# Where the attention's band mask is added to the scores: VectorE, in place in PSUM, in the stead of TensorE products

## The reference, cut to what matters

```python
valid = (jnp.abs(q_pos[:, None] - k_pos[None, :]) <= WINDOW) & (k_pos >= 0) & (k_pos < S)
s_win = jnp.einsum('bqkgd,bnkd->bkgqn', qb, kb).astype(jnp.float32) * scale
s_win = jnp.where(valid, s_win, MASK_VALUE)
s_ctx = jnp.einsum('bqkgd,bckd->bkgqc', qb, k_ctx).astype(jnp.float32) * scale
probs = sink_softmax(jnp.concatenate([s_ctx, s_win], axis=-1), sink)
o = (jnp.einsum('bkgqc,bckd->bqkgd', probs[..., :n_ctx], v_ctx.astype(jnp.float32))
     + jnp.einsum('bkgqn,bnkd->bqkgd', probs[..., n_ctx:], vb.astype(jnp.float32)))
```

## Time and profile before

| | |
|---|---|
| median of 3 runs | 2247.52 us (2244.53 to 2247.78) |
| the profiled execution's own time | 2246.7 us |
| its span, first to last instruction | 2245.1 us |
| PE busy | 2146.2 us (96%) |
| DVE busy | 1493.3 us (67%) |
| ACT busy | 1131.6 us (50%) |
| POOL busy | 368.8 us (16%) |
| attention, from its first scores to its last values | about 130.7 to 284.3 us |

### The profile page before, as it was taken

The page is one execution under the profiler, slowest core; times in us unless marked ns, Lnnn a source line. Parts: engine busy times, 40 slices in busy tenths (PEclk is TensorE's granted clock), DMA queues, the critical chain, the costliest instruction groups (busy, mean ns, idle before and its releaser), DMA issues.

```text
span 2245.1 us, 33136 instructions
## 1 busy us (share of the span) xinstructions
PE 2146.2 (96%) x12156; PEld 1715.7 (76%) x12157; DVE 1493.3 (67%) x1391; ACT 1131.6 (50%) x1278; POOL 368.8 (16%) x247
## 2 busy tenths in 40 slices
PE   6999999999999999799799999999999999999994
PEld 4876688887888888678677788888888887666882
DVE  3456656667457544789566645459999997555984
ACT  4135536222224522377555534347888885445872
POOL 0030004999991000100000000000000000000001
PEclk8999999999999999799899999999999999999997
DMA  8472022555443222399577755559999996557974
GB/s 328 195 293 83 1 97 100 188 189 200 168 179 120 76 93 102 142 375 371 197 275 271 306 197 184 193 183 410 367 395 378 384 370 251 211 218 269 380 292 158
DMA packets 78098, 515.87 MB, mean 230 GB/s; under 512 B 9008, under 2 KB 9264, under 8 KB 20944
## 3 DMA queue, kind: packets, MB, share of 16 engines
q1 hardware_dynamic: 61696, 442.85, 51.3%
q0 software_dynamic: 16336, 72.11, 8.5%
HBM read 482.41 MB, written 32.51 MB: 229 GB/s over the span
## 4 chain that ended last, share of the span: by engine, by line
PE 88%; DVE 6%; issue 2%; ACT 1%; DMA 1%; SPq 0%; POOL 0%; DVEq 0%; ACTq 0%; POOLq 0%
PE ps L1851 25%; PE ps L1853 24%; PE ps L1852 24%; PE ps L2232 3%; PE ps L2296 2%; PE ps L603 2%; PE ps L558 2%; PE ps L614 2%; PE ps L2278 1%; DVE lo L1191 1%; PE ps L1910 1%; PE ps L562 1%; DVE fl L1495 1%; DMA raw_pair<-w_mod 1%; PE ps L2029 0%
## 5 line engine op out<-in xcount | busy, mean ns | idle before, releaser
L1851 PE MATMUL ps<-ah,hi 128*128 128x512 f32 (+1 forms) x768 | 286.8, 373 | 5.7 <-DVE al L1356 2.4
L1853 PE MATMUL ps<-ah,lo 128*128 128x512 f32 (+1 forms) x768 | 284.9, 371 | 0.0
L1852 PE MATMUL ps<-al,hi 128*128 128x512 f32 (+1 forms) x768 | 284.9, 371 | 0.0
L1439 DVE TENSOR_TENSOR lo<-raw,hi 128x2048 fp32r<-128x2048 f32 x112 | 255.8, 2284 | 0.0
L1439 DVE TENSOR_TENSOR loa<-raw_pair,hia 128x2048 fp32r<-128x2048 f32 x112 | 251.1, 2283 | 1.1 <-ACT hia L960 1.1
L1439 DVE TENSOR_TENSOR lob<-raw_pair,hib 128x2048 fp32r<-128x2048 f32 x112 | 251.7, 2283 | 0.0
L960 ACT ACTIVATE hia<-raw_pair 128x2048 fp32r<-128x2048 f32 x112 | 214.4, 1915 | 49.9 <-DMA raw_pair<-w_moe 49.8
L1191 DVE TENSOR_TENSOR lo<-raw_pair,hi 128x2048 fp32r<-128x2048 f32 x59 | 183.8, 3118 | 80.0 <-ACT hi L848 78.5
L960 ACT ACTIVATE hi<-raw 128x2048 fp32r<-128x2048 f32 x112 | 214.8, 1918 | 11.1 <-DMA raw<-w_moe 11.1
L1851 PE MATMUL ps<-hia,xth 128*128 128x512 f32 x504 | 204.2, 405 | 16.2 <-issue 14.6
L960 ACT ACTIVATE hib<-raw_pair 128x2048 fp32r<-128x2048 f32 x112 | 215.0, 1921 | 1.0 <-DMA raw_pair<-w_moe 0.9
(11 more groups left out here) (309 smaller groups left out, 4050.0 us busy)
## 6 DMA issues: line engine op xcount, KB each, us to landing
raw_pair<-w_moe SPq DMA_DIRECT2D x224, 1024.0 KB, 6.7
raw<-w_moe SPq DMA_DIRECT2D x112, 1024.0 KB, 6.8
raw_pair<-w_pre SPq DMA_DIRECT2D x59, 1024.0 KB, 4.8
raw_pair<-w_mod SPq DMA_DIRECT2D x20, 1024.0 KB, 7.2
raw_pair<-w_mod POOLq DMA_DIRECT2D x14, 1024.0 KB, 5.2
rawm<-w_mod POOLq DMA_DIRECT2D x14, 1024.0 KB, 5.5
dispatched_x<-zt POOLq DMA_DIRECT2D x22, 512.0 KB, 10.8
xg<-dispatched_x POOLq DMA_DIRECT2D x8, 1024.0 KB, 11.3
```

What stands on the lines that cost most here:

```text
L1439: dve.tensor_tensor(LO_OF[j], raw8(r), HI_OF[j].bitcast(F32), ALU.subtract).then_inc(raw_used[r], 1)
L1851: pe.matmul(outp, wh, ah, start=first, stop=False, skip_group_check=True)
L1852: pe.matmul(outp, wh, al, start=False, stop=False, skip_group_check=True)
L1853: return pe.matmul(outp, wl, ah, start=False, stop=last, skip_group_check=True)
```

## The change

The identity `IDR`, its ACT copy and the mask products are gone from PE. The mask tile becomes plain fp32. DVE adds it in place in PSUM to the left and right chunks of both heads, with one TENSOR_TENSOR per pair before the maximum: 128x512 elements in a middle block, 128x256 in an edge block, the mask broadcast over the two heads. In middle blocks head 0 now has its window keys in the order left, mid, right (before: left, right, mid), so that the four masked chunks have a regular stride; the scores that PE starts with there are the right chunk's. The copy of the last two transposes (middle blocks) moves from DVE to ACT, behind the two exponentials of its step and ahead of `es`, `rrow` and `ah`. The semaphore counts follow.

```diff
         def attention_act(act, first_done):
...
                         act.activation(PR[2 * (q % 2) + f][:, 0:BLK * n_keys(q)], score_head(q, f), ACT.Exp,
                                        bias=NM[:, h:h + 1], scale=SCALE, accum_out=LSUM[:, h:h + 1]).then_inc(pr_ready, 1)
+                if 0 <= p < NPAIR and len(turns(p)) == 3:
+                    act.wait_ge(pt_full, turns_before(p) + 3)
+                    act.activation(PTS[p % 2][:, 8:10, :], turned(8, 10), ACT.Copy).then_inc(pta_ready, 1)
...
         def attention_dve(dve, tn, late):
...
-                    for g, (a, b) in enumerate(turns(p)[1:]):
-                        dve.wait_ge(pt_full, turns_before(p) + 2 + g)
-                        dve.tensor_copy(PTS[p % 2][:, a:b, :], turned(a, b)).then_inc(ptd_ready, 1)
+                    dve.wait_ge(pt_full, turns_before(p) + 2)
+                    dve.tensor_copy(PTS[p % 2][:, 4:8, :], turned(4, 8)).then_inc(ptd_ready, 1)
...
+                    if not edge(s // 8):
+                        dve.wait_ge(window_full, s - 7)
                     dve.wait_ge(s_full, s + 1)
+                    link(dve.tensor_tensor(masked_at(s), masked_at(s), masks_for(s), ALU.add))
                     link(dve.tensor_reduce(NRM[:, cols_], score_pair(s), AX.X, ALU.max, negate=True))
...
         def attention_pe(pe, second_done):
...
-                def masked(outs, sides):
-                    return pe.matmul(outs, IDR[:], MASK[:, sides], start=False, stop=True, skip_group_check=True)
...
                     for f in range(2):
-                        part(f, 2, 2, win_keys)
-                    side = slice(BLK, 2 * BLK) if b == 0 else slice(0, BLK)
-                    for f in range(2):
-                        at = score_at(s, f, 3 if b == 0 else 2)
-                        ins = masked(PSF[:, at:at + BLK], side)
+                        ins = part(f, 2, 2, win_keys)
                 else:
-                    part(0, 4, 1, K[:, kp, b * BLK:(b + 1) * BLK]).then_inc(mid_done, 1)
+                    part(0, 4, 1, win_keys[:, 2 * BLK:3 * BLK]).then_inc(right_done, 1)
                     part(1, 3, 2, ctx_keys)
                     part(0, 0, 2, ctx_keys)
-                    pe.wait_ge(mid_done, s - 7)
-                    part(1, 0, 3, win_keys)
-                    part(0, 2, 2, win_keys.rearrange("p (c n) -> p c n", c=3)[:, 0:3:2, :])
-                    at = score_at(s, 0, 2)
-                    masked(PSF[:, at:at + 2 * BLK], slice(0, 2 * BLK))
-                    at = score_at(s, 1, 0)
-                    ins = masked(PSF[:, at:at + 3 * BLK].rearrange("p (c n) -> p c n", c=3)[:, 0:3:2, :],
-                                 slice(0, 2 * BLK))
+                    pe.wait_ge(right_done, s - 7)
+                    part(1, 0, 3, win_keys).then_inc(window_full, 1)
+                    ins = part(0, 2, 2, win_keys[:, 0:2 * BLK])
```

More of the change, by code:

```diff
@@ L168, in program @@
         SILC = put("silc", [P, KD, 2], F32)
-        IDR = put("idr", [P, P], F32R)
         NRM = put("nrm", [P, NH], F32)
@@ L185, in program @@
         VC = put("vc", [P, 2, 256], F32, r2 + 26624)
-        MASK = put("mask", [P, 2 * BLK], F32R, r2 + 28672)
+        MASK = put("mask", [P, 2 * BLK], F32, r2 + 28672)
         PR = [put(f"pr{i}", [P, NKEY], F32, r2 + 29696 + 2560 * i) for i in range(4)]
@@ L312, in program @@
         dve_step = sem("dve_step")
-        silc_ready, idr_ready = sem("silc_ready"), sem("idr_ready")
+        silc_ready, window_ready = sem("silc_ready"), sem("window_mask_ready")
         xz_ready = sem("xz_ready")
@@ L317, in program @@
         kv_ready, rope_done = sem("kv_ready"), sem("rope_done")
-        mid_done, s_full, nm_ready, pr_ready = sem("mid_scores_done"), sem("scores_full"), sem("max_ready"), sem("probs_ready")
+        window_full = sem("window_scores_full")
+        right_done, s_full, nm_ready, pr_ready = sem("right_scores_done"), sem("scores_full"), sem("max_ready"), sem("probs_ready")
         pt_full, pta_ready, ptd_ready, av_done = map(sem, ("pt_full", "pta_ready", "ptd_ready", "av_done"))
@@ L437, in key_order @@
                 return [CTX0, CTX1, LEFT, MID]
-            return [LEFT, MID, RIGHT, CTX0, CTX1] if f else [CTX0, CTX1, LEFT, RIGHT, MID]
+            return [LEFT, MID, RIGHT, CTX0, CTX1] if f else [CTX0, CTX1, LEFT, MID, RIGHT]
         def turns(p):
@@ L446, in turns_before, with masked_at, masks_for @@
             return sum(len(turns(i)) for i in range(p))
+        def masked_at(s):
+            at = score_at(s, 0, 0)
+            if edge(s // 8):
+                c = 3 if s // 8 == 0 else 2
+                both = PSF[:, at:at + 8 * BLK].rearrange("p (f o c n) -> p f o c n", f=2, o=1, c=4)
+                return both[:, :, :, c, :]
+            heads = PSF[:, at + 2 * BLK:at + 8 * BLK].rearrange("p (f c n) -> p f c n", f=2, c=3)
+            return heads[:, :, 0:3:2, :]
+        def masks_for(s):
+            sides = MASK[:].rearrange("p (o c n) -> p o c n", o=1, c=2)
+            if edge(s // 8):
+                c = 1 if s // 8 == 0 else 0
+                return sides[:, :, c:c + 1, :].to_broadcast([P, 2, 1, BLK])
+            return sides.to_broadcast([P, 2, 2, BLK])
         def turned(a, b):
@@ L502, in link @@
                 dve.wait_ge(dve_step, tn.n("step"))
+            dve.wait_ge(window_ready, 1)
             for s in range(NPAIR + 4):
@@ L543, in attention_pe @@
         def attention_pe(pe, second_done):
-            pe.wait_ge(idr_ready, 2)
             pe.wait_ge(rope_done, 8)
@@ L624, in attention_pe @@
                     if p >= 1:
-                        pe.wait_ge(pta_ready, p)
-                        pe.wait_ge(ptd_ready, turns_before(p) - p)
+                        pe.wait_ge(pta_ready, turns_before(p) - p)
+                        pe.wait_ge(ptd_ready, p)
                     turn(p, 0)
@@ L635, in attention_pe @@
                 if 0 <= p < NPAIR:
-                    pe.wait_ge(pta_ready, p + 1)
+                    pe.wait_ge(pta_ready, turns_before(p) - p + 1)
                     turn(p, 1)
@@ L650, in attention_pe @@
                 if 0 <= p < NPAIR and len(turns(p)) == 3:
-                    pe.wait_ge(ptd_ready, turns_before(p) - p + 1)
+                    pe.wait_ge(ptd_ready, p + 1)
                     turn(p, 2)
@@ L867, in _ @@
             act.activation(SILP[:, :, 0:2], sm("cc").rearrange("p (k v) -> p k v", v=2), ACT.Silu).then_inc(silc_ready, 1)
-            act.activation(IDR[:], ident, ACT.Copy).then_inc(idr_ready, 1)
             def mod_row(p):
@@ L907, in _ @@
             act.wait_ge(mask_in, 16)
-            act.activation(MASK[:], MASKF[:], ACT.Copy).then_inc(idr_ready, 1)
+            act.activation(MASK[:], MASKF[:], ACT.Copy).then_inc(window_ready, 1)
             def deviation(n):
```

## The result

| | before | after |
|---|---|---|
| median | 2246.67 us (4 runs, 2244.53 to 2247.78) | 2261.93 us (4 runs, 2258.28 to 2264.53) |
| ratio after / before | | 1.0072, 95% [1.0059, 1.0084] |
| span of the profiled execution | 2245.1 us | 2260.3 us |
| mean granted clock | 0.978 | 0.973 |

The changed kernel is 15 us slower. The forecast was 2240.7 with a range up to 2248.5, so it missed in sign and in size. The attention became about 6 us shorter. The loss is in the experts, where the forecast did not look.

The account below looks back on a forecast made before the run. PE was taken to bound the kernel (88% of the chain), with a possibly late DVE/ACT loop. Gains of 1.2 (block 0), 3.5 (middle) and 2.1 (block 3) sum to 6.8 us: 2246.7 to 2239.9, plus 0.8 gives 2240.7; range 2235.5 to 2248.5.

Parts of the forecast that it names:

- The step that failed: Behind the attention: later stages start when it ends, so its gain or loss carries to the end in full.
- Mask off PE and one pass on DVE: Attention: PE sheds up to 11.3 us of mask products; DVE's add costs +0.73 us per middle step, +0.45 per edge step.
- the two-pass bound: DVE's add, high end: two passes, 1.37 us in a middle step and 0.84 in an edge step.
- Middle blocks: Attention's middle blocks: `nt` 0.24 us later behind `rrow`; each two-step period loses 0.44 of 10.07, 3.5 us gained.
- The tie that I saw at the exponentials: Middle blocks, odd step: ACT's copy behind the exponentials ends at T + 6.16, PE needs it at T + 6.27.
- Rival 2: Attention: the DVE and ACT loop replaces PE as bound; 2246.5 us, or 2250 with two-pass adds; 0.26 including only streaming gone.
- rival 1: Attention: PE is not held back, 11.3 us comes less about 2, so 9.3 gained, 2238 us; chance 0.15.
- Edge block 3: Attention's block 3: PE waits 0.07 to 0.1 us per two steps; 2.6 less 0.5 for the last pair, 2.1 gained.
- Block 0: Attention's first block: 6 x 0.37 saved on PE less two DVE adds of 0.45 in the chain; 1.2 us gained.
- Rival 3, the clock: Block 0: longer PE stalls keep the clock at 1.2 GHz over 11.3 us more PE work; 2252 us, chance 0.11.
- The rule of the Trainium skill that I weighed: PE in the attention: short pauses between matmul groups can repeatedly drop the clock, so waits cost more than their length; small chance.
- ACT's copy: Middle blocks: a free ACT copies the last transposes in about DVE's time, 0.38 us, 16 times; no gain, no loss.

Follow-up runs that it names:

- e9: The padded changed kernel (128 idle PE instructions ahead of the experts) with the last transposes' copy back on DVE, the add kept: 2238.62 us, ratio to before 0.9973.
- e8: The padded changed kernel (128 idle PE instructions ahead of the experts) with ACT's copy of the last transposes behind `rrow`: 2235.23 us, ratio to before 0.9952.
- e10: The kernel before, mask products kept on PE and no pad, with only the last transposes' copy moved to ACT: 2245.85 us, ratio to before 1.0007.
- e5: The changed kernel with 128 idle wait instructions added to PE ahead of the experts, putting the loop back at before's place: 2241.88 us, ratio to before 0.9976.
- e2: The changed kernel with PE's expert loop aligned to offset 136 of a 256-instruction block: 2380.32 us, ratio to before 1.0595.
- e3: The kernel before with PE's expert loop aligned to offset 136 of a 256-instruction block: 2388.67 us, ratio to before 1.0638.
- offset 8: PE's expert loop aligned to slot 8 of a 256-instruction block: changed kernel 2254.76 us (ratio to before 1.0034), kernel before 2260.16 us (1.0062).
- offsets 136 and 40: PE's expert loop aligned to those slots of a 256-instruction block: 136 in the changed kernel 2380.32 us, in before 2388.67; 40 in the changed kernel 2360.32.
- e6: The kernel before with 128 idle wait instructions added to PE ahead of the experts, moving the loop: 2269.05 us, ratio to before 1.0101.
- e11: e8 with a pad of 64 instructions instead of 128, moving the experts' loop: 2258.43 us, ratio to before 1.0060.

## Why the prediction was wrong

**The step that failed** is the last sentence of its first part, "What lies behind the attention starts when it ends, so I carry a gain or loss there to the end in full". Data and buffers do behave so: 9.0 us of lead stood at the end of the first expert, 7.5 of it since the attention's end. PE's code does not. The change takes 128 instructions from PE's stream and so moves everything behind them by half a block of 16 KB. With that, 7 packets of the experts' code were loaded a second time at the third expert, and its step became 23.9 us longer. None of the rivals had this, though before's own trace has the 12.65 us stall at the second expert, of which the prediction says nothing.

The terms, one by one:

- *Mask off PE and one pass on DVE*: right. 0.695 and 0.428 us against 0.69 and 0.42; the two-pass bound fell.
- *Middle blocks*: right in mechanism (`nt` behind ACT's `rrow`), period 9.49 against 9.63, stage 4.3 us against 3.5. The tie that I saw at the exponentials was not one: after's odd step has no wait of PE there. Rival 2 did not come, neither in its period nor in its two-pass add, and rival 1's full 0.68 a period was reached only by e9 (10.07 to 9.38, 0.69) and passed by e8 (0.84), which also takes DVE's copy out of the loop.
- *Edge block 3*: 2.3 us against 2.1, with a period of two steps shorter by 0.53 and not 0.64. The last pair's wait was 0.89 where before's was 0.58.
- *Block 0*: wrong in sign, 0.5 us lost and not 1.2 gained. The two waits of the earlier trace rows grew as said, to 1.16 and 1.77. But the clock fell twice (136 to 142 and 156 to 162 us) where it fell once before: the mean over 130 to 173 us is 0.92 and not 0.96. By e9 one fall is worth 1.2 to 1.5 us of block 0, so the second one is most of the 1.7 us that are missing; 0.2 to 0.5 stay open.
- *Rival 3, the clock*: its mechanism came, in seven of the eight profiled executions with the new attention; it was worth 1.2 to 1.5 us in place of over 11. My sign that "a clock under 0.94 in 130 to 173 us would make it wrong" was met, and has almost nothing to do with the loss. The rule of the Trainium skill that I weighed (short pauses making the clock fall again and again) did not bear on the middle blocks: clock 1.00 over 80.6 us.
- *ACT's copy*: the prediction took the copy itself at nothing, and the delay of `rrow` behind it at 0.24 us a period, 1.9 in eight. The direction of that delay was right and its size too large: 1.2 us with the mask on PE (e10), 0.7 with the add on DVE (e9's 74.34 to e5's 75.04). Behind `rrow` the copy was not nothing either but a gain of 1.3 (e9 to e8).

The sum for the attention, 6.8, stands against 5.9 to 6.1 measured in after, and the pairs at equal place of the code give 4.2 to 8.4. Without the move of the code the time would have been in the forecast's range: e5's 2241.88 lies within 1.2 us of 2240.7. Part of that is luck: the forecast starts from 2247.5 and takes off 6.8, while before measured 2246.11 in e5's set of runs and the gain there was 4.2, and block 0's missing 1.7 us were in part made up by the middle blocks and block 3.

A page bears on the cause. The Trainium skill, "Runtime: NRT & Kernel Launch", "Instruction fetch mechanics", says that an engine's instruction memory is refilled in blocks of 16 KiB, 256 instructions, and that a taken branch to a place outside the window that it holds stalls until the block is there. This case's traces agree: e2's 65 packets are 1.06 MB, 16 KB each, and the stalls stand at the first product of an expert or of the stage behind the loop, which PE reaches by a branch. The page also gives TensorE room for 2048 instructions, by which a loop of 1756 would be loaded once. In before it was, by the 46 packets of the whole execution; but e2 and e3 loaded code again for nearly every expert (65 packets).

**Open.** What decides between one stall of 12 us and several of up to 32: three places reached without alignment (13, 141 and 205 by my count) gave one, two and two stalls, offset 8 two, offsets 136 and 40 one at nearly every expert, and no rule that I tried fits all. That the packets were PE's is inferred: from who stood still, and from 46 packets in all where PE's compiled stream is 45.8. A stall at the second expert is in every version (10.6 to 13.0 us, and 21.6 to 21.8 at offsets 136 and 40). In before six packets start between 1076.1 and 1090.4 us, around this stall, and none of its packets is in excess of one loading of the stream; so it looks like the first loading of that code. No run tried to remove it.

## What to carry to other kernels

A change that adds or removes instructions ahead of a loop or branch moves the code behind it, and in these runs that alone was worth up to 143 us of 2250 (e3 against before). Look for "issue" stalls at the first instruction behind a branch together with packets of the instruction queue, and judge a change of a few us only at equal place of the code (a pad of idle waits gives it), else it is the place that is measured. When an operation is moved into an engine's stream, put it behind the ones whose results are awaited sooner: with the add on DVE, the same copy cost 0.7 us of the middle blocks ahead of `rrow` (74.34 to 75.04) and gained 1.3 behind it (74.34 to 73.01).

## What the runs showed of the hardware

- PE stood still for up to 32.5 us at a time while 16 KB packets of code arrived (6 or 7 packets with a stall of 21 us, 11 with one of 32.5), and had half the clock for some 6 us behind one of 21 us.
- Moving the loop by 64 or 128 instructions changed the time by 20 to 23 us (e5 to after, e6 to before, e11 to e8), in steps of a whole stall.
- One and the same sequence in block 0 ran with the clock falling never (e9) or twice (e5), 34.65 or 37.55 us: a difference of 3 us between two profiles of this kernel can be the clock's alone. Among thirteen profiled executions block 0 had one fall in all five of the old attention and two in seven of the eight of the new one.
- An add that reads and writes PSUM in place costs what an operation out of PSUM costs: 0.695 us for 128x512, 0.428 for 128x256.
